# Block products in two up projections, and a re-ordered pooling stage

## The reference, cut to what matters

```
mod = c_act @ ada_w[l] + ada_b[l];  sh1, sc1, g1, sh2, sc2, g2 = split(mod, 6)
h = x * (1 + sc1) + sh1
y = even_mixer(h) if l == 0 else pool_mixer(h)
x = layer_norm(ALPHA * x + g1 * y);  h = x * (1 + sc2) + sh2
u, v = split(h @ w_up, 2)                   # [512,1024] @ [1024, 2*2816]
uc = conv_b + sum_j pad(u)[:, j:j+T] * conv_w[j]
x = layer_norm(ALPHA * x + g2 * ((silu(uc) * v) @ w_down))

pool_mixer: for group gi (256 channels), window w in (2, 4, 8, 16):
    pooled = (sum of the last w tokens) / min(t + 1, w) - x
    y[gi] = pooled @ w_grp[gi];   y * scale
```

## Time and profile before

| | |
|---|---|
| Time, three runs | 2724.70, 2726.26, 2719.39 us; median 2724.7 |
| Profiled execution | 2716.38 us, span 2715.1 us |
| Mean granted TensorE clock | 0.969 |
| Busy share of the span | PE 93%, PEld 55%, DVE 48%, ACT 27%, POOL 3% |

### The profile page before, as it was taken

One profiled execution on the slowest core, in us unless ns is written; L12 is line 12 of the kernel. 1 busy time (PEld: TensorE's weight loads), 2 busy tenths in 40 slices (PEclk: granted clock), 3 DMA queues, 4 the chain that ended last, 5 costly groups with the idle time before them and its releaser, 6 DMA issues. The chain is left out here.

```text
span 2715.1 us, 35385 instructions
## 1 busy us (share of the span) xinstructions
PE 2537.2 (93%) x15484; PEld 1497.4 (55%) x15484; DVE 1303.5 (48%) x2129; ACT 728.4 (27%) x1357; POOL 88.2 (3%) x157
## 2 busy tenths in 40 slices
PE   7998989999996999999999999999998698999997
PEld 3575434444442444444456686776867663555973
DVE  3874343333116455551246958768595213232442
ACT  1323230000003200010144445455544403200231
POOL 2000100000000000000000000000000000000000
PEclk9998999999998999999999998999999898999999
DMA  7222424444211344431120100000000021111002
GB/s 302 93 94 85 164 100 155 155 155 174 95 72 41 119 150 152 153 126 64 69 112 17 49 5 32 19 18 34 3 32 17 3 108 62 62 47 62 32 32 93
DMA packets 41051, 227.71 MB, mean 84 GB/s; under 512 B 4609, under 2 KB 4737, under 8 KB 24641
## 3 DMA queue, kind: packets, MB, share of 16 engines
q1 hardware_dynamic: 20304, 140.55, 14.3%
q0 software_dynamic: 20016, 82.79, 8.6%
q10 hardware_dynamic: 576, 2.11, 0.2%
HBM read 219.13 MB, written 6.29 MB: 83 GB/s over the span
## 5 line engine op out<-in xcount | busy, mean ns | idle before, releaser
L301 PE MATMUL ps<-G,ring 128*128 128x512 f32 x704 | 303.3, 592 | 0.0
L609 PE MATMUL ps<-H,ring 128*128 128x512 f32 x672 | 295.2, 592 | 0.0
L604 PE MATMUL ps<-H,ring 128*128 128x512 f32 x672 | 295.2, 592 | 0.0
L1847 PE MATMUL ps<-H,ring 128*128 128x256 f32 (+1 forms) x832 | 271.4, 487 | 7.7 <-ACT LW L2064 5.4
L301 PEld LDWEIGHTS ps<-G,ring 128*128 128x128 f32 x704 | 133.8, 190 | 167.9 <-issue 167.9
L1847 PEld LDWEIGHTS ps<-H,ring 128*128 128x128 f32 x832 | 157.4, 190 | 115.2 <-issue 91.6
L609 PEld LDWEIGHTS ps<-H,ring 128*128 128x128 f32 x672 | 127.7, 190 | 160.7 <-issue 155.9
L604 PEld LDWEIGHTS ps<-H,ring 128*128 128x128 f32 x672 | 127.7, 190 | 160.7 <-issue 160.7
L301 PE MATMUL ps<-H,ring 128*128 128x512 f32 (+1 forms) x480 | 181.5, 535 | 0.9 <-DVE ls_tmp L2725 0.9
L462 DVE SCALAR_TENSOR_TENSOR R<-ps,mod,XA 128x512 f32<-128x512 f32 x24 | 18.0, 751 | 266.4 <-PE ps L301 250.9
L623 ACT COPY U<-ps 128x512 f32<-128x512 f32 x44 | 25.8, 586 | 425.0 <-PE ps L604 420.6
(11 more groups left out here) (535 smaller groups left out, 4066.8 us busy)
## 6 DMA issues: line engine op xcount, KB each, us to landing
ada_late<-ada_rest POOLq DMA_DIRECT2D x104, 512.0 KB, 4.0
ring<-w_up SPq DMA_DIRECT2D x44, 1024.0 KB, 4.9
ring<-w_down SPq DMA_DIRECT2D x16, 1408.0 KB, 6.0
ring<-od_in SPq DMA_DIRECT2D x16, 1024.0 KB, 4.8
ring<-ev_in SPq DMA_DIRECT2D x15, 1024.0 KB, 5.0
ada_early<-ada_rest POOLq DMA_DIRECT2D x24, 512.0 KB, 4.6
ada_first_sb<-ada_first SPq DMA_DIRECT2D x8, 1024.0 KB, 16.2
ring<-ab_in SPq DMA_DIRECT2D x7, 1024.0 KB, 5.9
```

Of the source, the lines that this page charges most:

```text
L301: mm = pe.matmul(k.ps[:, (n % deep) * nb + b, 0:tn], wv[:, kk, a * P:(a + 1) * P], rhs[:, kk, t0:t0 + tn], start=(kk == 0), stop=(kk == kt ...
L604: mm = pe.matmul(k.ps[:, b, :], wv[:, kk, 0:P], k.H[:, kk, 0:T], start=(kk == 0), stop=(kk == DT - 1))
L609: mm = pe.matmul(k.ps[:, b + 1, :], wv[:, kk, P:2 * P], k.H[:, kk, 0:T], start=(kk == 0), stop=(kk == DT - 1))
L1847: mm = pe.matmul(k.ps[:, bank + b, 0:tn], wv[:, kk, (i % 2) * P:(i % 2 + 1) * P], k.H[:, kk, t0:t0 + tn], start=(kk == 0), stop=(kk == DT ...
```

## The change

Up projections. A slab's 256 output columns (u and v), its 1024 inputs (even and odd tiles) and the 512 tokens (two halves) are cut in two each. The 2x2 block product is done with seven products instead of eight (Strassen's scheme in Winograd's form). Each product is four matmuls of 128x256, so a slab has 28 of these instead of 16 of 128x512. VectorE forms four sums of weight blocks for each slab (each 512 columns), eight sums of activations once per layer, and puts the products together with seven additions of 256 columns. ScalarE copies product 1 and takes over the first tap of the convolution. A slab uses four PSUM banks, two slabs in flight.

```diff
-EARLY, LATE = 3, 8
+EARLY, LATE = 3, 4
+def left_sums_dve(k, l, n):
+    v, A, S = k.nc.vector, left_blocks(k, l, n), k.LS[n % 2]
+    v.wait_ge(*k.when("slab", k.slab(f"w_up{l}", n)))
+    ... (n >= 2: products (l, n-2, 3); n == 1: norm "x" DT-1)
+    v.tensor_tensor(S[:, 2], A[0, 0], A[1, 0], ALU.subtract)
+    settled(k, v.tensor_tensor(S[:, 0], A[1, 0], A[1, 1], ALU.add))
+    settled(k, v.tensor_tensor(S[:, 1], S[:, 0], A[0, 0], ALU.subtract))
+    v.tensor_tensor(S[:, 3], A[0, 1], S[:, 1], ALU.subtract)   # "left sums"
+def right_sums_dve(k, l, h):      # waits norm "h" 4h+3, then four more of 512
+def ffn_pe(k, l):
+    first = ((1, A[0, 0], B[0, 0]), (2, A[0, 1], B[1, 0]))
+    middle = ((6, S1, R1), (5, S0, R0))
+    third, late = (3, S3, B[1, 1]), ((7, S2, R2), (4, A[1, 1], R3))
+    n == 0: wait left sums; 1 and 3 with the tiles of H; 2;
+            for h in 0, 1: wait right sums h, half of 6, 7, 4; then 5
+    n > 0:  wait slab, "ffn v" n-2; first -> products 0; wait left sums;
+            middle -> products 1; third, late[0] -> products 2;
+            late[1] -> products 3
 def ffn_act(k, l):
+        a.copy(k.P1[:, n % 2, :], product(k, n, 1))            # "first product"
+        a.wait_ge(*k.when("ffn u", l, n))
+        a.activation(C, U[2:T + 2], ACT.Identity, bias, scale) # "ffn tap"
         a.activation(C, C, ACT.Silu)
 def ffn_dve(k, l):
+    if l == 0:
+        v.wait_ge(*k.when("c2"))
     v.memset(k.U[:, :, 0:2], 0.0)
-    v.wait_ge(*k.when("c2"))
+    for h in range(2): right_sums_dve(k, l, h)
     for n in range(FT):
+        if n + 1 < FT: left_sums_dve(k, l, n + 1)
+        U[first half]  = first + p(2)                # after "first product"
+        X0 = first + p(6); X1 = X0 + p(5)            # after products 1, settled
+        U[second half] = X1 + p(3); X2 = X0 + p(7)   # after products 2
+        V = X2 + p(4), X2 + p(5)                     # after products 3
+        v.wait_ge(*k.when("ffn tap", l, n))
         two scalar_tensor_tensor of the convolution
+        for j in ADA_UP[l][n]: ada_tile_dve(k, j)
         v.wait_ge(*k.when("ffn silu", l, n))
-        v.tensor_tensor(k.G[:, n, :], C, k.ps[...], ALU.mult)
+        v.tensor_tensor(k.G[:, n, :], C, V[:], ALU.mult)
```

```diff
-"pool": (6, 7, 4, 5, 2, 3, 0, 1)
+"pool": (0, 1, 6, 7, 4, 5, 2, 3)
 def pool_dve(k):
-        for g in ((3, 2), (), (1,), (), (0,), (), (), ())[n]:
+        for g in ((3,), (), (2,), (), (1,), (), (), ())[n]:
             pooled_dve(k, g)
         ... evacuate row n
+        if n == 5: add rows 4 and 5, add their squares
     norm_scalars_dve(k, 1, 0)
-    mean, four less_mean, wait "rstd", eight normal
+    left_sums_dve(k, 1, 0)
+    shifted_norm_dve(k, st)
 def pool_pe(k):
+    pe.wait_ge(*k.when("pool weights"))
     ... two matmuls for row n
+        if n in (3, 5): for m in (n - 3, n - 2): pool_sums_pe(k, m)
-    eight row sums, then eight sums of squares
+    the two added pairs, then pool_sums_pe for 6 and 7
```

More of the change, by code:

```diff
@@ L491, in rows_act @@
     for n in range(5, DT):
+        if late and n == DT - 1:
+            late(k)
         a.wait_ge(*k.when("evac", name, 0, n))
@@ new lines, in right_sums_dve @@
+def right_sums_dve(k, l, h):
+    v, R = k.nc.vector, k.RS4
+    v.wait_ge(*k.when(("norm", l, 0), "h", 4 * h + 3))
+    B = {(e, s): right_block(k, e, s, 2 * h, 2 * h + 2) for e in range(2) for s in range(2)}
+    t1, t2, t3, t4 = (R[:, j, 2 * h:2 * h + 2, :] for j in range(4))
+    v.tensor_tensor(t3, B[1, 1], B[0, 1], ALU.subtract).then_inc(*k.says(DVE))
+    settled(k, v.tensor_tensor(t1, B[0, 1], B[0, 0], ALU.subtract))
+    settled(k, v.tensor_tensor(t2, B[1, 1], t1, ALU.subtract))
+    v.tensor_tensor(t4, B[1, 0], t2, ALU.subtract).then_inc(*k.says(DVE, "right sums", l, h))
@@ L591, in ffn_pe @@
         pe.wait_ge(*k.when("slab", g))
+        if n >= 2:
+            pe.wait_ge(*k.when("ffn v", l, n - 2))
         if n == 0:
[L593 to L597, removed]
@@ L598, in ffn_pe @@
-            mv.then_inc(*k.says(PE, "ffn mm v", l, n))
+            pe.wait_ge(*k.when("left sums", l, n))
+            for i in range(4):
+                pe.wait_ge(*k.when(st, "h", 2 * i))
+                times(n, *first[0], i)
+                pe.wait_ge(*k.when(st, "h", 2 * i + 1))
+                times(n, *third, i)
+            for i in range(4):
+                mm = times(n, *first[1], i)
+            mm.then_inc(*k.says(PE, "products", l, n, 0))
+            for h in range(2):
+                pe.wait_ge(*k.when("right sums", l, h))
+                for j, terms in ((0, middle[0]), (2, late[0]), (3, late[1])):
+                    for i in range(2 * h, 2 * h + 2):
+                        mm = times(n, *terms, i)
+                    if h and j:
+                        mm.then_inc(*k.says(PE, "products", l, n, j))
@@ L599, in ffn_pe @@
+            for i in range(4):
+                mm = times(n, *middle[1], i)
+            mm.then_inc(*k.says(PE, "products", l, n, 1))
             k.mark(PE, "slab used", g)
             continue
[L601 to L607, removed]
@@ L608, in ffn_pe @@
-        for kk in range(DT):
-            mm = pe.matmul(k.ps[:, b + 1, :], wv[:, kk, P:2 * P], k.H[:, kk, 0:T], start=(kk == 0), stop=(kk == DT - 1))
-        mm.then_inc(*k.says(PE, "ffn mm v", l, n))
+        for terms in first:
+            for i in range(4):
+                mm = times(n, *terms, i)
+        mm.then_inc(*k.says(PE, "products", l, n, 0))
+        pe.wait_ge(*k.when("left sums", l, n))
+        for terms in middle:
+            for i in range(4):
+                mm = times(n, *terms, i)
@@ L611, in ffn_pe @@
+        mm.then_inc(*k.says(PE, "products", l, n, 1))
+        for terms in (third, late[0]):
+            for i in range(4):
+                mm = times(n, *terms, i)
+        mm.then_inc(*k.says(PE, "products", l, n, 2))
+        for i in range(4):
+            mm = times(n, *late[1], i)
+        mm.then_inc(*k.says(PE, "products", l, n, 3))
         k.mark(PE, "slab used", g)
@@ L673, in between @@
             norm_scalars_dve(k, l, 1)
+            v = k.nc.vector
+            v.wait_ge(*k.now(DVE))
+            bias_sum_dve(k)
+        if n == 7 and l == 0:
+            bias_shift_dve(k)
         if n == 5 and l == 1:
@@ L1438, in pool_dve @@
             .then_inc(*k.says(DVE, "evac", "pool", 0, n))
-    norm_scalars_dve(k, 1, 0)
[L1440 to L1446, removed]
-def pool_act(k):
[L1451 to L1456, removed]
+        if n == 5:
+            v.wait_ge(*k.now(DVE))
+            v.tensor_tensor(k.pool_a[:, 0, 0:T], k.R[:, 4, :], k.R[:, 5, :], ALU.add).then_inc(*k.says(DVE, "pool sum"))
+            v.wait_ge(*k.when(st, "square", 5))
+            v.tensor_tensor(k.pool_b[:, 0, 0:T], k.pool_sq[:, 4, :], k.pool_sq[:, 5, :], ALU.add).then_inc(*k.says(DVE, "pool square sum"))
```

183 lines of the change are left out of this document (144 added, 39 removed).

## The result

| | before | after |
|---|---|---|
| Time, median of the runs of one comparison | 2722.05 us (2713.93 to 2726.26) | 2652.65 us (2649.03 to 2653.31) |
| Ratio to before, 95% interval | | 0.9747 [0.9731, 0.9762] |
| Profiled execution; its span | 2716.38; 2715.1 us | 2653.14; 2651.8 us |
| Mean granted TensorE clock | 0.969 | 0.964 |

The account below looks back on a forecast made before the run. TensorE, busy 93% of the span, was taken as the bound. Terms -68.9 + 13.4 - 11.5 + 1.5 = -65.5 us took the profiled execution from 2716.4 to 2650.9 and the median from 2724.7 to 2659, range 2642 to 2700.

Parts of the forecast that it names:

- TensorE bounds the slabs: Up projections, slabs 1 to 21 of both layers: 56 passes, 12.09 us a slab instead of 13.73, saving 68.9 us.
- VectorE follows: Up slabs: VectorE's queue takes 10.2 us in layer 0 and 10.6 in layer 1, under TensorE's 12.09; bounds 9.8 to 13.1.
- Weight loads stay hidden: Up projections: the 0.19 us weight load disappears beside each 256-column pass, which takes 0.216 us.
- rival D: Up slabs: weight loads not hidden, a pass 0.41 us, a slab 22.7 us, 3106 us in all; chance 0.01.
- Slab 0 of layer 0: 13.4 us lost: weight sums ahead of the mean, TensorE idle 8 us behind the c2 wait, then half clock.
- Rival C: No penalty at c2 in layer 0's slab 0 and a better pooling chain: 10 us more won, 2648; chance 0.12.
- Down projection: Down rows stay at 18.9 us; the moved ada tiles and norm sums hide in VectorE's idle time, cost nothing.
- Pooling: Pooling stretch: mean to first scaling saves 9.2 us, mean 2.3 earlier, last row as before; together 11.5 us saved.
- Slab 0 of layer 1: No c2 wait, but right sums follow VectorE's last scaling; ends at about +17 instead of 15.6, 1.5 us lost.
- A: Up slabs: VectorE sets the pace at 13.1 us a slab, 42 us of gain go, about 2701; chance 0.14.
- B: Up slabs: half-rate sums, dearer PSUM reads and waits make VectorE 14.6 us a slab, slower at 2765; chance 0.05.
- E: Pooling chain gains nothing because TensorE at low clock limits it: 10 us less gained, 2670; chance 0.10.

Follow-up runs that it names:

- Experiment 9: Changed kernel with product 4 computed twice in slabs 1 to 21 of both layers, so eight products a slab; 2724.71 us, ratio 1.0017.
- experiment 3: Changed kernel with two more settled weight sums of 512 columns in VectorE's queue for each slab; 2659.0 us, ratio 0.9773.
- experiment 4: Changed kernel with six more settled weight sums of 512 columns in VectorE's queue for each slab; 2747.97 us, ratio 1.0097.
- experiment 5: Changed kernel with the moved ada tiles back in layer 1's up projection, two in each slab; 2662.57 us, ratio 0.9791.
- experiment 6: The changed kernel again, unedited, as reference for a later comparison; 2650.35 us, ratio 0.9746.
- Experiment 1: Changed kernel with VectorE's wait for c2 moved from ahead of layer 0's activation sums to ahead of its first ada tiles; 2644.26 us, ratio 0.9719.
- experiment 7: Changed kernel with the c2 wait moved to the first ada tiles and layer 0's slab-0 weight sums ahead of the last attention row; 2636.98 us, ratio 0.9700.
- Experiment 8: On top of experiment 7: pooling row sums and squares pre-added on VectorE, layer 1's slab-0 weight sums in two halves; 2640.3 us, ratio 0.9702.

## Why the prediction was right, step by step

- **TensorE bounds the slabs; 12.09 us each.** Right to the hundredth, and the size of the gain with it: -34.6 us a layer against -34.4. Experiment 9 shows that TensorE's passes set it, experiment 3 that 1.44 us more on VectorE don't.
- **VectorE follows.** Right: 9.8 us a slab in layer 0 and 9.9 in layer 1 (874.53 to 884.47), under the 10.2 and 10.6 forecast. The additions move the queue on by 2.7 us instead of 2.9, the product with v by 0.61 instead of 0.69 (399.05 to 399.66). The half-rate weight sum, 1.22 us as the upper bound, isn't there: it takes 0.685. Experiments 3, 4 and 5 show where the other side lies.
- **Weight loads stay hidden**, and rival D falls: PEld is busy 223.50 us beside 253.88 us of PE, and the passes go at 0.216 us, as in the earlier trace rows. The rule of the Trainium skill, page "TensorE: Matmul & The Clock Gate", Part 3 (packing small matmuls), by which only loads to other rows overlap, would have made a slab 22.7 us; the measurement decides against it for these loads of all rows. (22.7 us is an estimate, by that rule and with the prices of the earlier trace rows.)
- **Slab 0 of layer 0, +13.4.** Measured +13.1, by the two mechanisms named: the first right sum at 380.34 where I had the end of the wait at 380.8, a gap of 9.19 us where I said 8, since TensorE had done its products by 373.9 and not 375.5, and passes at half rate behind it. The row that gave 5.2 us of half clock carried over well to this execution: the first right-sum passes took 0.47 us each, and the clock was 0.51 for 5.2 us. In experiment 6 it was back sooner and the same stage cost 12.3 instead of 13.1. Experiment 1 takes 12.0 us of it away, experiment 7 another 0.7. Rival C was wrong about the changed kernel; experiment 1 shows what it would have been worth, 12 us rather than 10.
- **Down projection, 0.** Measured +0.3. VectorE still idles 11.50 us before the last row's evacuation, where it was 20.03 in the kernel before, and 6.70 us before row 6's, where it was 14.47. So that row, with the norm sums and three tiles, is the tight one, as I had it.
- **Pooling, -11.5.** Measured -10.4. Mean to first scaling gained 9.2, exactly as read from layer 0's norm. Last row to mean gained 2.6 (6.93 to 4.30 us) where I said 2.3. The term that I missed is the last row itself, which I had as before: it comes 42.8 us after the down projection's, 1.5 later than the 41.3 of before. I had only weighed TensorE's half rate for the sums behind the rows; it delays the rows too, since the two groups at half rate and the sums between rows leave VectorE waiting 3.01 us. Experiment 8 shows it for the sums: with fewer of them among the rows, and the first two groups as in experiment 6 (5.8 and 5.4 us), VectorE has no wait for TensorE left ahead of its last two rows (2.75 us in experiment 6) and the stage falls from 53.4 to 51.1 us. For the clock there are only the two profiles of the same kernel: in experiment 6 the last row came 0.7 us later than before and not 1.5, and the stage gained 11.2.
- **Slab 0 of layer 1, +1.5.** Measured +0.6. I had TensorE wait for the first right sums; they are done at 866.6, and TensorE, still busy with product 2, takes them at 867.43 without a wait.
- **The rivals.** A and B fall with VectorE at 9.8 and 9.9 us a slab, E with the 10.4 us that the pooling gained.
- **The sum and the median.** The stages of the table sum to -65.5 us, the forecast to the tenth, but that is luck: misses cancel (pooling +1.1, slab 0 of layer 1 -0.9), and in experiment 6, the same kernel, the same stages sum to -67.1. Outside them the execution was 2.2 us longer, so it took 2653.1 where the working had 2650.9. For the median I then added 8.3 us, the distance of before's profiled execution from its median. In the comparison that distance was 5.7 us for before and -0.5 for after. This is the one term that was clearly mis-sized: it puts the forecast 8.8 us too high, and with the 2.2 leaves the 6.4 between 2659 and 2652.65.

What stays open is why the recurrent stage varies, below; no experiment was made on it.

## What to carry to other kernels

Seven products for eight pay nearly the eighth that they save, here 12.0% of the slabs' time, as long as VectorE holds its additions under TensorE's shorter slab: sum its queue per slab first, and move foreign work off it to a stage with cover. A wait that is hoisted to the head of an in-order queue is priced by what stands behind it and by the half clock that TensorE has after the gap; here one line cost 12 us in a change that brings 69, and moving it and four sums gives 2637 us, the lowest median here, with experiment 8 equal to it within the intervals. And when a stage that a change doesn't touch varies by 10 us, judge parts of the change by the distance between instructions at the ends of their own stage, not by totals.

## What the runs showed of the hardware

The recurrent stage, from layer 1's last down matmul to the first output projection, has the same instructions in all ten kernels, and took 817.3 to 827.5 us in their profiles (820.3 before, 821.7 after, 826.3 in experiment 1, 826.1 in experiment 3). It goes along with the granted clock of the stage: 0.96 in the two shortest (817.3 and 817.9 us), 0.95 from 820.3 to 822.1, 0.94 from 826.1 to 826.4, 0.93 in the longest. Busy by stretch, the whole stage: experiment 7, then experiment 8.

```profile
1271.30:2089.20 817.90, 753.72 (x10175) 564.20 (x10173) 541.95 (x909) 398.81 (x838) 4.30 (x8) 0.96 0.09 30
```

```profile
1266.80:2093.20 826.40, 764.52 (x10175) 574.59 (x10173) 541.96 (x909) 398.92 (x838) 4.30 (x8) 0.94 0.08 30
```

The same 10175 passes keep TensorE busy 10.8 us longer at 0.94 than at 0.96, while VectorE is busy 541.95 and 541.96 us. It isn't the kernel alone that decides: the four runs of experiment 7 alone go from 2635.59 us at a mean clock of 0.969 to 2644.75 at 0.963. What decides how often TensorE goes to its half level in this stage was not tested.
